# Gate weight sums of a Strassen-like product: where they are parked, and where they are split

## The reference

```
for i in range(2):
    mix = pool and gating heads (layer 0) or a gated short convolution (layer 1)
    x = layer_norm(ALPHA * x + mix)
    hid = square(relu(x @ ffn_w1[i]))                      # 1024 -> 4096
    x = layer_norm(ALPHA * x + hid @ ffn_w2[i])            # 4096 -> 1024
    gate = sigmoid(x @ ple_gate_w[i])                      # 1024 -> 1024
    x = x + gate * (p[i] @ ple_w[i])                       # 256 -> 1024
```

## Time and profile before

| | |
|---|---|
| runs, us | 2057.12, 2057.95, 2059.17 (median 2057.95) |
| profiled execution, us | 2063.47 |
| its span, us | 2061.7 |
| mean granted TensorE clock | 0.997 |
| VectorE, ScalarE, GpSimd busy | 68%, 43%, 37% |
| gate_parts stores | 40 of 512 KB, 4.4 us to landing |
| gate_parts loads | 20 of 1024 KB, 4.8 and 7.0 us to landing |
| loads of the quarters | 16 of 512 KB, 4.9 us to landing |

### The profile page before, as it was taken

One profiled execution on the slowest core, in us unless ns is written; L12 is line 12 of the kernel. 1 busy time (PEld: TensorE's weight loads), 2 busy tenths in 40 slices (PEclk: granted clock), 3 DMA queues, 4 the chain that ended last, 5 costly groups with the idle time before them and its releaser, 6 DMA issues.

```text
span 2061.7 us, 25116 instructions
## 1 busy us (share of the span) xinstructions
PE 2036.8 (99%) x9341; PEld 1689.1 (82%) x9341; DVE 1405.0 (68%) x1721; ACT 890.9 (43%) x1283; POOL 763.4 (37%) x505
## 2 busy tenths in 40 slices
PE   9999999999999999999999999999999999999999
PEld 9888788888888888787888888788888888887877
DVE  4744775655666868676887669775655666777595
ACT  3112465455544445352433343654444543445541
POOL 5212257777702000110367650268877412000200
PEclk9999999999999999999999999999999999999999
DMA  6121123444589896434122238033443599886343
GB/s 190 38 66 41 41 75 129 159 159 147 203 288 390 301 321 224 167 112 153 42 77 87 88 114 308 21 117 139 160 155 135 207 380 383 281 296 226 113 174 123
DMA packets 201366, 352.19 MB, mean 171 GB/s; under 512 B 14401, under 2 KB 72861, under 8 KB 198685
## 3 DMA queue, kind: packets, MB, share of 16 engines
q1 hardware_dynamic: 190432, 320.92, 44.5%
q10 hardware_dynamic: 10812, 29.67, 3.9%
HBM read 258.78 MB, written 91.75 MB: 170 GB/s over the span
## 4 chain that ended last, share of the span: by engine, by line
PE 79%; DVE 11%; issue 3%; POOL 3%; ACT 2%; DMA 1%; DVEq 0%; ACTq 0%; POOLq 0%
PE bank_a L2735 15%; PE bank_a L2737 15%; PE bank_a L2736 15%; PE bank_b L2735 10%; PE bank_b L2737 10%; PE bank_b L2736 10%; POOL op_lo L1457 2%; DVE hop_lo L2521 1%; DMA w_raw<-in_ffn_w_dram 1%; DVE wop_lo L2524 1%; PE bank_a L2774 1%; PE bank_b L2774 1%; POOL op_sum L1548 1%; DVE xt_lo L2021 1%; DVE xt_lo L2221 1%
## 5 line engine op out<-in xcount | busy, mean ns | idle before, releaser
L1444 POOL TENSOR_TENSOR w_lo<-raw,w_hi 128x512 fp32r<-128x512 f32 x84 | 118.3, 1440 | 694.6 <-ACT w_hi L1569 694.5
L1457 POOL TENSOR_TENSOR op_lo<-op_sum,op_hi 128x512 fp32r<-128x512 f32 x151 | 224.5, 1503 | 33.4 <-ACT op_hi L1891 27.5
L1891 ACT CAST op_hi<-op_sum 128x512 fp32r<-128x512 f32 x151 | 93.8, 621 | 328.9 <-POOL op_sum L1548 87.9
L1856 ACT CAST hop_hi<-h_raw 128x1024 fp32r<-128x1024 f32 x124 | 130.3, 1051 | 231.2 <-PE bank_a L2737 134.7
L2735 PE MATMUL bank_a<-wop_hi,hop_hi 128*128 128x512 f32 x576 | 224.4, 390 | 0.4 <-DVE resid L2543 0.4
L2736 PE MATMUL bank_a<-wop_lo,hop_hi 128*128 128x512 f32 x576 | 224.3, 389 | 0.0
L2737 PE MATMUL bank_a<-wop_hi,hop_lo 128*128 128x512 f32 x576 | 224.3, 389 | 0.0
L2521 DVE TENSOR_TENSOR hop_lo<-h_raw,hop_hi 128x1024 fp32r<-128x1024 f32 x124 | 152.0, 1226 | 97.4 <-ACT hop_hi L1856 97.2
L1457 POOL TENSOR_TENSOR op_lo<-w_raw,op_hi 128x512 fp32r<-128x512 f32 x115 | 164.1, 1428 | 116.9 <-ACT op_hi L1891 115.8
L2735 PE MATMUL bank_b<-wop_hi,hop_hi 128*128 128x512 f32 x432 | 171.0, 396 | 7.4 <-DVE resid L2546 7.4
L2737 PE MATMUL bank_a<-xt_hi,op_lo 128*128 128x512 f32 x456 | 177.6, 390 | 0.0
(11 more groups left out here) (275 smaller groups left out, 4940.7 us busy)
## 6 DMA issues: line engine op xcount, KB each, us to landing
w_raw<-in_ffn_w_dram SPq DMA_DIRECT2D x144, 512.0 KB, 6.7
h_raw<-h_spill SPq DMA_DIRECT2D x112, 512.0 KB, 6.5
h_spill<-h_tile SPq DMA_DIRECT2D x170, 256.0 KB, 2.1
w_raw<-in_ffn_w_dram SPq DMA_DIRECT2D x112, 256.0 KB, 3.5
gate_parts<-park_r ACTq DMA_DIRECT2D x40, 512.0 KB, 4.4
w_hi<-gate_parts SPq DMA_DIRECT2D x10, 1024.0 KB, 4.8
w_lo<-gate_parts SPq DMA_DIRECT2D x10, 1024.0 KB, 7.0
w_raw<-in_od_w_in_dram SPq DMA_DIRECT2D x40, 256.0 KB, 3.4
```

Of the source, the lines that this page charges most:

```text
L1444: pool.tensor_tensor(lo, raw[:, n % NRAW, :], hi.bitcast(F32), ALU.subtract).then_inc(lo_split, 1)
L1457: pool.tensor_tensor(by_four(op_lo[s]), operand_raw(tr, b, op), by_four(op_hi[s]).bitcast(F32), ALU.subtract).then_inc(op_low, 1)
L1856: act.copy(hop_hi[k][:, :, :], h_raw[a.hop_chunk(i)][:, :, :]).then_inc(ahead_hi, 1)
L1891: act.copy(by_four(op_hi[s]), operand_raw(tr, b, op)).then_inc(op_high, 1)
```

## The change

The parks are shorter and later, and they hold plain sums: no high and low parts, no B22. Each half now has four steps from item 24 on: at step 0 four quarters are loaded, at step 1 VectorE makes the four sums, at step 2 ScalarE stores them. The first half stands at items 24 to 27, the second at items 28 to 31; its loads wait until the first half's stores are done, as before. In the gates each sum is loaded once (1 MB) into a buffer of its own; B22 is loaded from the weight itself. ScalarE copies the high part into `w_hi` and VectorE writes the low part into `w_lo`, once the form that used them is done. VectorE's order is rearranged: the low parts of weights stand with those of the activations, and some affine steps stand later. The stores of residual tiles in layer 1 are left as they are.

The diff, cut to its core:

```diff
-GATE_X = ("S3a0", "S3a1", "S3b0", "S3b1", "S2r0", "S2r1", "S3l0", "S3l1", "S4a0", "S4a1", "S2l0", "S2l1",
-          "S1r0", "S1r1", "Xh0", "Xh1", "Xl0", "Xl1", "S4b0", "S4b1", "S4l0", "S4l1", "S1l0", "S1l1")
+GATE_X = ("S3a0", "S3a1", "S3b0", "S3b1", "S2r0", "S2r1", "T3l0", "T3l1", "S3l0", "S3l1", "S4a0", "S4a1",
+          "S2l0", "S2l1", "T2l0", "T2l1", "S1r0", "S1r1", "S4b0", "S4b1", "Xh0", "Xh1", "Xl0", "Xl1",
+          "S1l0", "S1l1", "T1l0", "T1l1", "S4l0", "S4l1", "B22l0", "B22l1", "T4l0", "T4l1")
-PARK_FROM, PARK_STEPS = 20, 13
+PARKED = ("T3", "T1", "T2", "T4")
+PARK_FROM, PARK_STEPS = 24, 4
+        gw_raw = {a: at(f"gw_raw{a}", [P, 4, HALF], a * K1) for a in (152, 160, 184)}
+        gate_home = dict(T3=gw_raw[160], T1=gw_raw[152], T2=gw_raw[184], T4=gw_raw[160], B22=gw_raw[184])
...
 SyncE, load_gate:
                 if name == "m1":
-                    gate_product_done(sp, st, "m1")
-                    part("T3", 0)
+                    last = heads[layer]["m4"]
+                    sp.wait_ge(b_full, last.gb + HT)
+                    part("T3")
+                    part("T1")
+                    sp.wait_ge(lo_split, st.heads["m2"].n("piece"))
+                    part("T2")
                 if name == "m2":
-                    sp.wait_ge(b_full, st.gb + HT + 1)
-                    part("T2", 1)
+                    gate_x_done(sp, layer, "T3l1")
+                    part("T4")
                 if name == "m7":
-                    gate_product_done(sp, st, "m7")
-                    part("T1", 0)
+                    gate_x_done(sp, layer, "T2l1")
+                    rows = ple_gate_w[layer][HALF:2 * HALF, HALF:2 * HALF].rearrange("(q p) n -> p q n", p=P)
+                    sp.dma_start(gate_home["B22"][:, :, :], rows).then_inc(gate_w_in[4], 16)
+                if name == "m6":
+                    gate_x_done(sp, layer, "T1l1")
                     rows = ple_w[layer][:, HALF:2 * HALF].rearrange("(q p) n -> p q n", p=P)
                     sp.dma_start(gp_raw[:, :, :], rows).then_inc(gate_w_in[5], 16)
                 if layer == 1 and name in ("m2", "p12", "p22", "p21"):      (unchanged)
                     ... for k in range(HT): sp.wait_ge(x_new, 2 * TT * layer + base + k + 1), then the store
...
 ScalarE, load_and_park:
+                    for tile, (i, j) in enumerate(((1, 1), (0, 1), (0, 0), (1, 0))):
+                        quarter(i, j, park[tile])
                 if s == 2:
+                    for k, (name, tile) in enumerate((("T3", 0), ("T1", 1), ("T2", 2), ("T4", 3))):
+                        park_done(act, st, name)
+                        act.dma_start(gate_dram[layer, k, :, 2 * m:2 * m + 2, :], park[tile][:, :, :]).then_inc(park_out, 16)
...
 ScalarE, gate_scalar:
+                def w_high(form, c):
+                    hi, _ = gate_weights(layer, c)
+                    gate_load_landed(act, layer, form)
+                    for m in range(2):
+                        act.copy(pair_of(hi, m), pair_of(gate_home[form], m)).then_inc(gate_high, 1)
   m2:  gate_product_done m1, w_high("T3", 0) before S3's high part
   m7:  gate_product_done m2, w_high("T2", 1) before S4's
   m6:  w_high("T1", 0) behind S1's
   m5:  gate_product_done m6, w_high("B22", 1) before m5's bank copies
   m3:  gate_product_done m5, w_high("T4", 0) before the sigmoids
...
 VectorE, park_vector:
                 if st.item == 1:
-                    low("B22h", 3, 0, 2)
+                    park_landed(dve, st, 4)
                     step(park[0], park[0], park[1], ALU.subtract)
+                    park_done(dve, st, "T3")
                     step(park[1], park[1], park[2], ALU.subtract)
+                    park_done(dve, st, "T1")
                     step(park[2], park[0], park[2], ALU.add)
+                    park_done(dve, st, "T2")
+                    step(park[3], park[3], park[2], ALU.subtract)
...
 VectorE, gate_vector:
                     gate_x_done(dve, layer, "S2r1")
+                    w_low("T3", 0)
                     x_low(s3[1], g_sum[80], s3[0], "S3")
...
                     gate11(1, 5)
-                    affine((2,))
-                    gate11(2, 6)
-                    affine((3,))
-                    gate11(3, 7)
+                    for k in (2, 3):
+                        sig_ready(f"s11{k}")
+                        times_bank(sig3[:, k % 3, :], "B", st.gb + 4 + k + 1, st.gb + 4 + k)
                 if name == "m7":
...
                     x_low(xt11[1], g_sum[48], xt11[0], "S2")
+                    w_low("T2", 1)
                     x_step(g_sum[168], g_sum[168], g_sum[176], ALU.add)
+                    x_step(g_sum[56], g_part, xt12[1].bitcast(F32), ALU.add, "S4a")
                     (X high and low, as before)
-                    x_step(g_sum[56], g_part, xt12[1].bitcast(F32), ALU.add, "S4a")
+                    gate_product_done(dve, st, "m7")
+                    x_low(s3[1], g_sum[168], s3[0], "S1")
+                    w_low("T1", 0)
                     x_low(xt12[1], g_sum[56], xt12[0], "S4")
                 if name == "m6":
-                    gate_product_done(dve, st, "m7")
-                    x_low(s3[1], g_sum[168], s3[0], "S1")
-                    affine(range(HT, HT + 2))
+                    for k in (2, 3):
+                        affine((k,))
+                        add_gated(sig3[:, k % 3, :], k, 0, f"n{k}")
+                    affine(range(HT, HT + 1))
                 if name == "m5":
-                    affine(range(HT + 2, TT))
+                    w_low("B22", 1)
+                    affine(range(HT + 1, TT - 1))
                     (m5's copies plus m7's banks, as before)
+                if name == "m3":
+                    w_low("T4", 0)
+                    affine(range(TT - 1, TT))
...
 TensorE, gate_product:
-                    gate_x_done(pe, layer, x_part)
-                    gate_part_landed(pe, layer, w_part)
+                    gate_x_done(pe, layer, {"m7": "S3l1", "m6": "T2l1", "m5": "T1l1", "m3": "B22l1", "m4": "T4l1"}[name])
```

More of the change, by code:

```diff
@@ L1013, in gate_product_done, with gate_load_landed @@
                 engine.wait_ge(b_full, head.gb + (2 * HT if name == "m2" else HT))
-        def gate_part_landed(engine, layer, name):
-            engine.wait_ge(gate_w_in[PARKED.index(name)], 32 * (layer + 1))
+        def gate_load_landed(engine, layer, name):
+            engine.wait_ge(gate_w_in[GATE_LOADS.index(name)], 16 * (layer + 1))
         def park_done(engine, st, name):
-            engine.wait_ge(park_step, gate_count(PARK_D, 2 * st.layer + st.half, name))
-        def park_high_done(engine, st, name):
-            engine.wait_ge(park_high, gate_count(PARK_A, 2 * st.layer + st.half, name))
+            engine.wait_ge(park_step, gate_count(PARKED, 2 * st.layer + st.half, name))
         def park_landed(engine, st, loads):
@@ L1028, in park_stored @@
         def park_stored(engine, st, groups):
-            engine.wait_ge(park_out, 32 * (len(PARKED) * (2 * st.layer + st.half) + groups))
+            engine.wait_ge(park_out, 16 * (len(PARKED) * (2 * st.layer + st.half) + groups))
         def by_four(ap):
@@ L1681, in quarter @@
                     act.dma_start(dst[:, :, :], rows.rearrange("(q p) n -> p q n", p=P)).then_inc(park_in, 16)
[L1683 to L1687, removed]
                 if s == 0:
@@ L1768, in gate_scalar @@
                 if name == "m5":
+                    gate_product_done(act, st, "m6")
+                    w_high("B22", 1)
                     gate_x_done(act, layer, "S1l1")
@@ L1808, in stage @@
                     load_and_park(st)
-                    form = {1: ("B22h", 2, 0), 4: ("T3h", 3, 0), 7: ("T1h", 3, 1), 8: ("T2h", 0, 2), 11: ("T4h", 3, 1)}.get(st.item)
-                    if form:
-                        name, dst, raw_w = form
-                        if name == "B22h":
-                            park_landed(act, st, 2)
-                        else:
-                            park_done(act, st, name[:2] + "r")
-                            park_stored(act, st, {"T3h": 1, "T1h": 2, "T2h": 2, "T4h": 3}[name])
-                        act.copy(park_r[dst][:, :, :], park[raw_w][:, :, :]).then_inc(park_high, 1)
                 if st.kind == "turn" and st.source == "ln" and st.ln % 2 == 1 and st.half == 0 and st.js[0] == 0:
-                    act.wait_ge(park_out, 32 * len(PARKED) * 2 * (st.layer + 1))
+                    act.wait_ge(park_out, 16 * len(PARKED) * 2 * (st.layer + 1))
                 if st.kind == "gx":
@@ L2222, in x_low, with w_low @@
                             .then_inc(gate_x, 1)
+                def w_low(form, c):
+                    hi, lo = gate_weights(layer, c)
+                    x_low(lo, gate_home[form], hi, form)
                 def affine(tiles):
@@ L2237, in add_bank, with times_bank, add_gated @@
                     dve.tensor_tensor(tile, tile, banks[ring][bank % RING][:, :], ALU.add).then_inc(gate_read, 1)
```

(11 more changed lines are left out.)

77 lines of the change are left out of this document (16 added, 61 removed).

## The result

| | before | after |
|---|---|---|
| median of the runs, us | 2058.16 (4 runs, 2057.12 to 2059.17) | 2069.88 (4 runs, 2068.67 to 2071.27) |
| profiled execution, us | 2063.47 | 2069.41 |
| its span, us | 2061.7 | 2067.5 |
| mean granted TensorE clock | 0.997 | 0.995 |

A forecast was written before the change was run, and what follows sets the result against it. TensorE, busy 2036.8 of 2061.7 us, bounds the kernel; only its standing still can change. -9.2 + 0.6 - 4.6 + 1.4 + 6.8 = -5.0, forecast 2053.0 us from a median of 2057.95, range 2049.5 to 2059.

The forecast's parts named there:

- Parks in items 24 to 31: MLPs, before m3: four park loads land after 10.6 us (9.3 to 11.9), nearly covered by VectorE's lead; +0.6 us.
- rival 1: MLP, item 29: parks land late, up to 4.5 us a layer, giving 2061.4; chance 0.14, of which 0.06 beyond 2062.1.
- Late parks go: MLPs, before m4: TensorE's stalls go with the late parks, 5.0 us in layer 0, 4.2 in layer 1; -9.2.
- Gates: Gates, both layers: VectorE's new order removes the waits before m6 and m5, 2.3 us per layer; -4.6.
- m3: Gates, layer 0: form m3 waits for B22's low part, behind affine steps on VectorE; +1.4 us (0.5 to 2.5).
- Layer 1's B22: Layer 1's gates: B22's load stands behind output stores on SyncE, TensorE stands 5.7 us before m3; +6.8 (5.5 to 9).
- Rival 4: After a stall of 5.7 us slow starts last longer than after 4: +1.5 us, 2054.5; chance 0.12.

The follow-up runs named there:

- the experiment on the burst: Changed kernel with two output stores moved behind the B22 load, and the parks' first half at items 20 to 23: 2058.91 us, ratio 0.9994.
- the second profile: The kernel before, unchanged, profiled once more: 2058.01 us, span 2056.3, clock 0.999.

## Why the prediction was wrong

**The step that failed** is the second of the change part by part, "Parks in items 24 to 31", +0.6. It named the right place, engine and order (VectorE, item 29, two preparations behind the sums, then the bank read). Its landing time was wrong, and the reckoning had 0.2 us of cover, so each us of error went onto the path. In layer 0:

| | forecast | measured |
|---|---|---|
| fourth load lands | 737.0 | 740.4 |
| sums end | 741.6 | 745.3 |
| first bank read ends | 746.8 | 750.5 |
| gap of TensorE, less one start | 0.3 | 3.9, and 1.7 of slow starts |

The 10.6 us to landing came from two loads that had the engines alone for about half of the earlier trace rows. The prediction read those rows as a near-even split with both queues at work; they are 64% to 34%, and both were at work for about one us of the four. The measured 13.6 is beyond even the 11.9 of the bound. Two things were left out: with six of SyncE's loads, issued from 723.0 to 729.2, next to them the parks get half, and the first half, which ends just before, pushes SyncE's loads into the same stretch (2.8 us, by the experiment on the burst). The two MLPs cost 5.5 and 7.1 us where 0.6 was charged. This was rival 1, for which 0.14 was given; its price, 4.2 us a layer, was below what came.

**Late parks go, -9.2.** The stalls did go. The sum was too large: the second profile has gaps of 2.7 and 2.8 us, which with slow starts is 6.8. The prediction set a profiled execution 5.3 us above the median against the median one for one, and that execution had longer stalls at this place. It also counted four slow starts where its own profile has thirteen behind layer 0's gap and six behind layer 1's (2.8 and 1.4 us, not 0.9 and 1.0), so that in that execution the stalls were worth 11.5 us, not 9.2. The cause is shown only as a whole: it isn't the slow loads alone, since a stall of this size stays with the loads cured and VectorE's parking work packed.

**Gates, -4.6, and m3, +1.4.** Both waits went; m3's is 0.9 us in layer 0. Layer 0's gates gave 1.2 us, 0.9 was the forecast. By these two steps the arithmetic with durations of single operations held within 0.5 us; with the affine steps put back it gave 12 for 9.1.

**Layer 1's B22, +6.8.** The forecast was a stall of 5.7 with the load at 950.1 in layer 0's times; measured are 5.73 us more than a normal start, and 2.6 of slow starts. Moving two stores brought back 8.6, of which 7.1 are this stall less what layer 0 has too. The mechanism and the stall's size are right; the slow starts were 1.1 in the sum. Rival 4 named the extra 1.5 us, but not for the right reason: slow starts don't last longer after the longer stall. After gaps of 5.2 and 6.0 us ten and twelve starts come at half the rate (seven after 6.0 with the parks at item 32), after gaps of 4.1 to 4.3 us eight to 13. The prediction, whose rows end early behind the gap, counted four.

Sum of the terms as measured: -6.8 before m4, +12.6 before m3, -4.6 and +1.2 in the gates, +8.3 for B22, +0.8 between the layers (not traced further): 11.5. The traces say 11.6.

## What to carry to other kernels

A block that waits for a transfer costs an in-order engine wait plus work, and the two must fit together into its lead over TensorE; a lead of 8 us hid 7.0 of wait or 4.6 of work, not both. So place such a block behind a read of banks that TensorE needs, not just ahead of it (here two preparations stood between), and ask of each place which flush comes next. A landing time read where the other queue was empty half of the time isn't one for four loads at once: add up the bytes that all queues want in the stretch. And before a stall of one profiled execution is booked as a saving, see how that execution stands to the median.

## What the runs showed of the hardware

The clock after a gap isn't fixed by the gap. In the version with the first half at items 20 to 23 two gaps of 2.71 us, one in each layer, ended differently (windows just behind the first and the second):

```profile
706.40:711.00 4.60, 4.56 (x13) 0.63 0.72 248
...
1769.60:1774.00 4.40, 4.37 (x19) 1.00 0.73 256
```

The same gap cost eight half-rate starts, 1.6 us, or none. Over all profiles no gap up to 1.9 us was followed by a fall, gaps of 2.7 to 3.4 us by none or by up to 13 slow starts (none after 3.41 and 13 after 3.40 us, in one execution, with the affine steps put back), and each above 3.5 us by at least seven. Between the two profiles of the kernel before, 5.5 us apart, slow starts at m4 are 2.5 us of the difference and the gaps themselves 2.2, so both make its runs spread; the four versions without a stall above 2 us in the MLPs and the gates have clock 0.999 or 1.000 in every run.
